# Second-layer expert weights issued from GpSimd's DMA queue, first-layer weights from SyncE's

## The chip, the cores and the metric

The kernel runs on one core of a Trainium2 chip. The metric is the time of the whole program on the device in microseconds (us), as the median of several executions. A trace of one profiled execution stands beside it. Engines are named as the profile names them: PE is TensorE, PEld its weight load, DVE is VectorE, ACT is ScalarE, POOL is GpSimd and SP is SyncE. SP computes nothing here: it issues DMAs. Its DMAs go to the queue that the profile calls q1, hardware_dynamic. DMAs that POOL issues go to q0, software_dynamic. Both queues are served by the same 16 DMA engines of the core.

## The reference

One inference step of a decoder layer on 304 tokens (16 meta tokens, 256 of a prompt, 8 sequences of 4): a layer norm, a mixer of three parallel head groups with one projection in and one out, and then a mixture of 32 experts, of which every token takes 4. The stage that matters here is that last one:

```python
top_val, top_idx = lax.top_k(logits, TOP_K)               # 4 of 32
def expert_block(args):
    xb, e = args
    hid = xb @ lp["moe_w1"][e] + lp["moe_b1"][e]          # 1024 x 2048
    gate = jnp.minimum(hid[:, :D_FF], SWIGLU_LIMIT)
    lin = jnp.clip(hid[:, D_FF:], -SWIGLU_LIMIT, SWIGLU_LIMIT)
    act = gate * jax.nn.sigmoid(SWIGLU_ALPHA * gate) * (lin + 1.0)
    return act @ lp["moe_w2"][e] + lp["moe_b2"][e]        # 1024 x 1024
```

All is float32. An expert has 8 MB of first-layer weights (w1) and 4 MB of second-layer weights (w2), and all 32 experts' weights are read once.

## The kernel before

The program is written engine by engine, with semaphores between the engines set by hand. The first 180 us are the mixer and the router. After that the experts are worked through in 16 pairs. Each expert of a pair takes up to 64 tokens (`CAP`).

**Pieces and slots.** The weights come in pieces of 2 MB, 128 partitions by 16 KB. An expert has `PIECES` = 6 of them: 4 of w1 (`W1P`) and 2 of w2. A pair is `PAIR` = 12 pieces, always in this order, and in this text they are numbered 0 to 11 within their pair: 0 to 3 are w1 of the first expert, 4 to 7 are w1 of the second, 8 and 9 are w2 of the first, 10 and 11 are w2 of the second. SBUF has a ring of `SLOTS` = 8 slots of one piece each. The pieces go through the slots in turn, so a piece may be requested once the piece eight before it has been used. PE counts used pieces on the semaphore `w_used`, and `room(k)` is the wait for it. The loader, `load_group`, loads two pairs per call (`GROUP` = 4 experts) and is called eight times, seven of them in a loop. SP issues all of the pieces, in order, into its one queue. The first eight are issued during the mixer (`load_first`, L454). All signals are per pair of slots: `w_full` for the first piece of two, `w_half` for the second.

**PE's order within a pair** (`pair`, L1870):

1. `first_layer(0, ...)` with pieces 0 to 3 (L1886). In its middle, after half of piece 1, stands `gather(1)`, which picks token columns for a later pair (L1855).
2. `combine`, which adds the pair before to the output (L1863, L1868), with `biases(1)` (L1770) in the middle of it.
3. `first_layer(1, ...)` with pieces 4 to 7. Between pieces 5 and 6 stands `inner(0)`, the transposes of the first expert's activations (L1911).
4. `gather(0)` (L1855), `biases(0)` (L1770), and the transposes of `put` (L1953).
5. `second_layer(0, ...)` with pieces 8 and 9 (L1901), `inner(1)` (L1911) between them, and `second_layer(1, ...)` with pieces 10 and 11 (L1901).

Before each piece PE waits for its `w_full` or `w_half`. After it PE counts `w_used` up.

**POOL.** It makes constants at the start, issues some small loads and the stores of the mixer's states, clears buffers at about 150 us, and then has nothing to do until two multiplications at the very end (L651, L652).

**The end.** After the last pair PE adds the last outputs (L1981, L1992). Then come the last layer norm on DVE and ACT, and the stores. SP issues the last norm's parameters, `ln2`, to the ring's first slots (L527, L528) once the last expert's first layer has been read. These follow the weights in q1.

Of the kernel before, what the change touches and what calls it, by code (L numbers as in the profile page):

```python
# [40 lines left out]
NE, TOPK = 32, 4  # L41
# [15 lines left out]
PIECES = 6  # L57
W1P = 4
PAIR = 2 * PIECES
SLOTS = 8  # L60
GROUP = 4
# [3 lines left out]
PASSES = -(-TOUT // CAP)  # L65
# [52 lines left out]
def build_kernel(nc, x_prompt, x_sample, state_conv_a, state_rglru, state_conv_b, state_gla, meta_tokens, ln0_g, ln0_b,  # L118
# [4 lines left out]
    with ExitStack() as ctx:  # L123
        def sb(name, shape, dt=F32):
            return ctx.enter_context(nc.sbuf_tensor(name, shape, dt))

        def sem(name):
            return ctx.enter_context(nc.semaphore(name))
# [18 lines left out]
        npass = sb("npass", [P, 1], I32)  # L147
# [173 lines left out]
        ld_moe = sem("ld_moe")  # L321
        w_full = [sem(f"w_full{s}") for s in range(SLOTS // 2)]
        w_half = [sem(f"w_half{s}") for s in range(SLOTS // 2)]
        w_used = sem("w_used")
        var_ready, std_ready = sem("var_ready"), sem("std_ready")
        ln0_stats, xhat_ready, h0_ready = sem("ln0_stats"), sem("xhat_ready"), sem("h0_ready")
# [21 lines left out]
        mask_ready, routed, y_started = sem("mask_ready"), sem("routed"), sem("y_started")  # L348
# [48 lines left out]
        def w2_piece(e, s):  # L397
            return moe_w2[0, bass.ds(e, 1), s * 4 * P:(s + 1) * 4 * P, :].rearrange("a (p t) c -> p (a t c)", t=4)

        def slots(s, n):  # L400
            return ring[:, s * SLOT:(s + n) * SLOT]
# [3 lines left out]
        def _(sp):  # L405
# [79 lines left out]

            def load_group(e, n, first=0):

                def expert(i):
                    return e + i if isinstance(e, int) else sp.snap(e + i)

                def room(k):
                    sp.wait_ge(w_used, PIECES * n + k - SLOTS + 1)

                for q in range(2):
                    for j in range(2):
                        for c in range(2):
                            k = PAIR * q + W1P * j + 2 * c
                            if k < first:
                                continue
                            ei = expert(2 * q + j)  # L500
                            src = [w1_half(ei, c, h) for h in range(2)]
                            room(k)
                            sp.dma_start(slots(k % SLOTS, 1), src[0]).then_inc(w_full[k // 2 % 4], 16)
                            room(k + 1)
                            sp.dma_start(slots(k % SLOTS + 1, 1), src[1]).then_inc(w_half[k // 2 % 4], 16)
                    for j in range(2):
                        k = PAIR * q + 2 * W1P + 2 * j
                        ei = expert(2 * q + j)
                        src = [w2_piece(ei, c) for c in range(2)]
                        room(k)  # L510
                        sp.dma_start(slots(k % SLOTS, 1), src[0]).then_inc(w_full[k // 2 % 4], 16)
                        room(k + 1)
                        sp.dma_start(slots(k % SLOTS + 1, 1), src[1]).then_inc(w_half[k // 2 % 4], 16)

            load_group(0, 0, SLOTS)
            with sp.Fori(1, NE // GROUP) as g:
# [3 lines left out]
            n_pass = sp.value_load(npass[0:1, 0:1], min_val=1, max_val=PASSES)  # L520
# [22 lines left out]
        def _(pool):  # L543
# [56 lines left out]
            for b in range(2):  # L600
                r = slice(NE * b, NE * b + NE)
# [29 lines left out]
            for n in range(NSEQ):  # L631
                r = WB - 1 + n * DSEQ
# [12 lines left out]
            st.do(pool.memset(posm[:, :, PASSES * NE:], -1.0), moe_cleared)  # L645
            st.do(pool.memset(eout[:, :, :], 0.0), moe_cleared)
            st.do(pool.memset(putT[:, :], 0.0), moe_cleared)

            pool.wait_ge(ld_lnq, 16 * 8)
            pool.wait_ge(sample_normed, 1)  # L650
# [841 lines left out]
        def _(pe):  # L1492
# [377 lines left out]
            def pair(q, gi, pi, first=False):  # L1870
                def first_layer(j, k0, k1):

                    for k in range(k0, k1):
                        f = (PAIR * q + W1P * j) // 2 + k // 4
                        if k % 4 == 0:
                            pe.wait_ge(w_full[f % 4], 16 * (gi * 3 + f // 4 + 1))
                        if k % 4 == 2:
                            pe.wait_ge(w_half[f % 4], 16 * (gi * 3 + f // 4 + 1))
                        if j == 0 and k < 4 and first:
                            pe.wait_ge(xT_first, k + 1)  # L1880
                        elif j == 0 and k % 4 == 0:
                            pe.wait_ge(xT_ready, 2 * pi + k // 4)
                        for b in range(2):
                            for h in range(2):
                                c = f % 4 * 2 * SLOT + k % 4 * MB1 + (2 * b + h) * 512
                                ins = pe.matmul(bank[b][64 * h:64 * h + 64, :], xT[:, q, k, j * CAP:(j + 1) * CAP],  # L1886
                                                ring[:, c:c + 512], start=False, stop=k == KT - 1)
                        if k % 2 == 1:
                            ins.then_inc(w_used, 1)

                def second_layer(j, k0, k1):

                    f = (PAIR * q + 2 * W1P + 2 * j) // 2
                    for k in range(k0, k1):
                        if k == 0:
                            pe.wait_ge(w_full[f % 4], 16 * (gi * 3 + f // 4 + 1))
                        if k == 4:
                            pe.wait_ge(w_half[f % 4], 16 * (gi * 3 + f // 4 + 1))
                        for h in range(2):
                            c = f % 4 * 2 * SLOT + k * D + h * 512  # L1900
                            ins = pe.matmul(bank[OUT_BANK[j]][64 * h:64 * h + 64, :],  # L1901
                                            actT[:, j, k % 4, (k // 4) * CAP:(k // 4 + 1) * CAP],
                                            ring[:, c:c + 512], start=k == 0, stop=k == KT - 1)
                        if k % 4 == 3:
                            ins.then_inc(w_used, 1)

                def inner(j):

                    pe.wait_ge(act_ready, 2 * pi + j + 1)
                    for k in range(4):  # L1910
                        ins = pe.transpose(bank[3][:, k * P:(k + 1) * P], l1[:, k:512:4], ident[:, :])  # L1911
                    ins.then_inc(actT_full, 1)

                first_layer(0, 0, 3)
                if first:
                    pe.wait_ge(xT_first, 4)
                gather(1)
                if first:
                    first_layer(0, 3, 6)
                    pe.wait_ge(gates_ready, 1)  # L1920
                    for t in range(3):
                        ins = pe.transpose(bank[3][0:NE, t * P:(t + 1) * P], gates[:, t, :], ident[:, :])
                    ins.then_inc(putT_full, 1)
                    first_layer(0, 6, KT)
                else:
                    first_layer(0, 3, KT)

                pe.wait_ge(putT_ready, pi + 1)
                pe.wait_ge(out_ready, 4 * pi + 1)
                combine(pi, 0)  # L1930
                combine(pi, 1)
                pe.wait_ge(bsel_ready, 2 * pi + 2)
                pe.wait_ge(g1_ready, 2 * pi + 1)
                pe.wait_ge(l1_ready, 2 * pi + 1)
                biases(1)
                pe.wait_ge(xT_ready, 2 * pi + 1)
                for c in range(2, NCOMB):
                    combine(pi, c)
                first_layer(1, 0, 4)
                inner(0)  # L1940
                first_layer(1, 4, KT)

                pe.wait_ge(pick_ready, pi + 3)
                pe.wait_ge(y_added, NCOMB * pi + 4)
                gather(0)
                pe.wait_ge(bsel_ready, 2 * pi + 3)
                pe.wait_ge(g1_ready, 2 * pi + 2)
                pe.wait_ge(l1_ready, 2 * pi + 2)
                biases(0)
                pe.wait_ge(put_ready, 2 * pi + 2)  # L1950
                pe.wait_ge(actT_ready, 2 * pi + 1)
                for t in range(3):
                    ins = pe.transpose(bank[3][:, t * P:(t + 1) * P], put[:, t, :], ident[:, :])  # L1953
                ins.then_inc(putT_full, 1)
                pe.wait_ge(y_added, NCOMB * pi + NCOMB)
                second_layer(0, 0, 4)
                pe.wait_ge(putT_ready, pi + 2)
                inner(1)
                second_layer(0, 4, KT)
                pe.wait_ge(actT_ready, 2 * pi + 2)  # L1960
                second_layer(1, 0, KT)

            for q in range(2):
                pair(q, 0, q, first=q == 0)
            pe.wait_ge(routed, 1)
            n_pass = pe.value_load(npass[0:1, 0:1], min_val=1, max_val=PASSES)
# [63 lines left out]
```

## Time and profile before

| | before |
|---|---|
| time, median of 3 runs | 1119.58 us (1119.24 to 1119.7) |
| the profiled execution's own time | 1117.23 us |
| its span in the trace | 1115.4 us |
| TensorE clock over the span | 0.993 of full speed |
| PE busy | 1074.2 us (96%) |
| DVE, ACT, POOL busy | 375.1, 164.1, 40.8 us |
| expert stage, first pair's first matmul to last pair's last | 180.9 to 1096.3 us |
| moved by DMA | 425.71 MB, of it 1.75 MB on q0 |

The span is what the instructions of the trace cover. The execution's own time is 1.8 us longer. "Busy" counts an engine's instructions, not how well they use it. "Idle before" in a row of the timeline is the time in which PE had nothing to do just before the row, with what ended it.

### The profile page before, as it was taken

The page shows a single profiled execution, that of the slowest core. Times are in us where ns is not written, and L with a number is a line of the kernel's source. Part 1 is how long each engine was busy: PE and PEld are TensorE (multiplying, and loading weights), DVE is VectorE, ACT ScalarE, POOL GpSimd, SP SyncE. Part 2 cuts the span into 40 slices and gives each one's busy share as a digit, 9 for nine tenths or more (in the row PEclk, how much of TensorE's full clock was granted, in tenths as well). Part 3 has the DMA queues.
Part 4 walks back from the last instruction along what each step waited for, and adds up shares of the span by engine and source line. Part 5 has one row for each costly group of instructions (what it writes and reads, how often), then busy time and mean ns, then how long its engine had stood idle before and what let it go on. Part 6 is the DMA issues. An engine that isn't in the chain of part 4 may idle for free.

```text
span 1115.4 us, 14027 instructions
## 1 busy us (share of the span) xinstructions
PE 1074.2 (96%) x5443; PEld 467.2 (42%) x5443; DVE 375.1 (34%) x941; ACT 164.1 (15%) x314; POOL 40.8 (4%) x101
## 2 busy tenths in 40 slices
PE   7999889999999999999999999999999999999996
PEld 4667545343434343434343333333333343434342
DVE  4797645313131313131313131223232313122134
ACT  4165622100100010001000100010101010101002
POOL 8000300000000000000000000000000000000000
PEclk9999989999999999999999999999999999999998
DMA  9534637999999999999999999999999999999993
GB/s 291 198 150 160 268 124 264 405 428 430 425 430 430 425 430 426 429 428 428 432 427 430 426 430 431 426 431 426 430 428 428 432 426 430 426 430 431 427 430 127
DMA packets 41642, 425.71 MB, mean 382 GB/s; under 512 B 6617, under 2 KB 13150, under 8 KB 17033
## 3 DMA queue, kind: packets, MB, share of 16 engines
q1 hardware_dynamic: 39729, 423.62, 90.6%
q0 software_dynamic: 1888, 1.75, 0.6%
q8 instruction: 16, 0.26, 0.1%
q14 instruction: 9, 0.07, 0.0%
HBM read 423.39 MB, written 2.17 MB: 382 GB/s over the span
## 4 chain that ended last, share of the span: by engine, by line
PE 73%; DMA 22%; DVE 2%; ACT 1%; POOL 1%; issue 0%; SPq 0%; DVEq 0%
PE bank L1886 34%; DMA ring<-in_moe_w_dram 20%; PE bank L1901 11%; PE bank L1507 7%; PE bank L1855 6%; PE bank L1868 5%; PE bank L1770 2%; PE bank L1534 1%; DMA out_dram<-ring 1%; PE bank L1911 1%; PE bank L1863 1%; PE bank L1739 1%; PE bank L1512 0%; DMA xt<-in_x_prompt_dram 0%; PE bank L1953 0%
## 5 line engine op out<-in xcount | busy, mean ns | idle before, releaser
L1886 PE MATMUL bank<-ring,hT 128*64 128x512 f32 x2048 | 454.9, 595 | 16.0 <-DMA ring<-in_moe_w_dram 16.0
L1886 PEld LDWEIGHTS bank<-ring,hT 128*64 128x64 f32 x2048 | 141.6, 137 | 300.3 <-issue 267.0
L1901 PE MATMUL bank<-ring 128*64 128x512 f32 x1024 | 226.8, 595 | 0.0
L1405 DVE TENSOR_SCALAR ring<-bank 128x512 f32<-128x512 f32 x32 | 22.1, 691 | 311.8 <-PE bank L1886 311.8
L1901 PEld LDWEIGHTS bank<-ring 128*64 128x64 f32 x1024 | 70.7, 137 | 132.6 <-issue 126.3
L1855 PEld LDWEIGHTS bank<-ring 128*128 128x128 f32 x768 | 88.1, 192 | 26.0 <-issue 26.0
L1422 DVE COPY ring<-bank 64x512 f32<-64x512 f32 x32 | 22.2, 694 | 219.3 <-PE bank L1901 219.3
L1855 PE MATMUL bank<-ring 128*128 128x128 f32 x768 | 94.2, 279 | 0.0
L1355 DVE TENSOR_SCALAR hT<-bank,ring 128x128 f32<-128x128 f32 x128 | 43.6, 402 | 130.4 <-PE bank L1855 130.4
L898 ACT ACTIVATE ring<-ring 128x512 f32<-128x512 f32 x32 | 20.1, 630 | 380.4 <-DVE ring L1405 380.4
L1868 PE MATMUL bank<-ring 128*128 128x512 f32 x128 | 63.5, 618 | 0.0
L902 ACT ACTIVATE ring<-bank 128x512 f32<-128x512 f32 x32 | 19.1, 597 | 248.4 <-PE bank L1911 248.4
L1507 PE MATMUL bank<-hT,ring 128*128 128x304 f32 (+1 forms) x208 | 53.4, 415 | 0.0
L1368 DVE TENSOR_TENSOR xt<-xt,bank 128x512 f32<-128x512 f32 x64 | 43.9, 686 | 5.8 <-PE bank L1868 5.5
L1507 PEld LDWEIGHTS bank<-hT,ring 128*128 128x128 f32 x208 | 39.2, 190 | 12.6 <-issue 0.4
L913 ACT ACTIVATE ring<-bank 64x512 f32<-64x512 f32 x32 | 18.9, 589 | 148.4 <-PE bank L1901 148.4
L1868 PEld LDWEIGHTS bank<-ring 128*128 128x128 f32 x128 | 21.7, 189 | 34.9 <-issue 34.9
L1770 PE MATMUL bank<-ring 32*64 32x512 f32 x264 | 35.9, 613 | 0.0
L651 POOL TENSOR_TENSOR ring<-ring 128x256 f32<-128x256 f32 x1 | 0.7, 722 | 958.9 <-ACT ring L930 958.9
L1739 PE MATMUL bank<-ring 128*128 128x512 f32 x64 | 32.6, 668 | 0.0
L1911 PEld LDWEIGHTS bank<-ident,ring 128*128 128x128 f32 x128 | 18.0, 210 | 26.0 <-issue 26.0
L1416 DVE TENSOR_SCALAR ring<-io,ring 128x64 f32<-128x64 f32 x96 | 24.1, 308 | 0.0
(322 smaller groups left out, 619.0 us busy)
## 6 DMA issues: line engine op xcount, KB each, us to landing
ring<-in_moe_w_dram SPq DMA_DIRECT2D x192, 2048.0 KB, 29.5
ring<-in_w_in_dram SPq DMA_DIRECT2D x5, 1536.0 KB, 13.4
ring<-in_w_out_dram SPq DMA_DIRECT2D x2, 2048.0 KB, 11.2
ring<-in_w_in_dram SPq DMA_DIRECT2D x1, 2048.0 KB, 13.7
xt<-in_x_prompt_dram SPq DMA_DIRECT2D x2, 512.0 KB, 4.3
lnbc<-in_ln_g_dram SPq DMA_DIRECT2D x2, 512.0 KB, 12.5
lnbc<-in_ln_b_dram SPq DMA_DIRECT2D x2, 512.0 KB, 12.8
ring<-in_state_gla_dram POOLq DMA_DIRECT2D x4, 144.0 KB, 5.5
```

Of the source, the lines that this page charges most:

```text
L1355: ins = dve.tensor_scalar(xT[:, parity, 4 * b + k, :], bank[(2, 5)[b]][:, k * 2 * CAP:(k + 1) * 2 * CAP], ln1c[:, 0, 4 * b + k:4 * b + k + ...
L1368: dve.tensor_tensor(dst, dst, bank[COMB_BANK[c]][:, :], ALU.add).then_inc(y_added, 1)
L1416: ins = dve.tensor_scalar(put[:, t, j * CAP:(j + 1) * CAP], io64[:, :], posm[:, t, bass.ds(n, 1)], gates[:, t, bass.ds(e, 1)], ALU.is_equa ...
L1422: dve.tensor_copy(eout[64 * j:64 * j + 64, 1, :], bank[OUT_BANK[j]][64:128, :]).then_inc(out_ready, 1)
L1507: ins = pe.matmul(out, a, b, start=n == 0, stop=n == len(pairs) - 1)
L1739: ins = pe.matmul(bk(f"P{t}{c}")[:, :], yT[:, k, cols[t][0]:cols[t][1]], wout[:, k, c * 512:(c + 1) * 512], start=k == 0, stop=k == KT - 1)
L1770: pe.matmul(bank[b][64 * h:64 * h + 64, :], bsel[e0:e0 + NE, j, :], b1_sb[e0:e0 + NE, h, :], start=True, stop=False)
L1855: ins = pe.matmul(out, xh[:, t, k * P:(k + 1) * P], pick[:, t, :], start=t == 0, stop=t == 2)
L1868: pe.matmul(out[:, :], putT[:, t * P:(t + 1) * P], eout[:, h, :], start=True, stop=True).then_inc(comb_full, 1)
L1886: ins = pe.matmul(bank[b][64 * h:64 * h + 64, :], xT[:, q, k, j * CAP:(j + 1) * CAP], ring[:, c:c + 512], start=False, stop=k == KT - 1)
L1901: ins = pe.matmul(bank[OUT_BANK[j]][64 * h:64 * h + 64, :], actT[:, j, k % 4, (k // 4) * CAP:(k // 4 + 1) * CAP], ring[:, c:c + 512], star ...
L1911: ins = pe.transpose(bank[3][:, k * P:(k + 1) * P], l1[:, k:512:4], ident[:, :])
```

## The change

SP's loader issues only the w1 pieces, with the same semaphores as before. POOL gets a loader of its own, `load_second`, which issues the w2 pieces. It stands behind POOL's clearing of the buffers and ahead of its two last multiplications. The w2 pieces have semaphores of their own, `w2_full` and `w2_half`. PE waits for those in `second_layer`, and the counts that it waits for are adapted. The slots, the order of the pieces in the ring and the `w_used` count at which each may be requested stay as they are. Nothing changes in what PE, DVE and ACT compute.

```diff
@@ load_group, on SP
-                    for j in range(2):
-                        k = PAIR * q + 2 * W1P + 2 * j
-                        ei = expert(2 * q + j)
-                        src = [w2_piece(ei, c) for c in range(2)]
-                        room(k)
-                        sp.dma_start(slots(k % SLOTS, 1), src[0]).then_inc(w_full[k // 2 % 4], 16)
-                        room(k + 1)
-                        sp.dma_start(slots(k % SLOTS + 1, 1), src[1]).then_inc(w_half[k // 2 % 4], 16)
...
@@ GpSimd, behind the memset of putT
+            def load_second(e, n):
+
+                def room(k):
+                    pool.wait_ge(w_used, PIECES * n + k - SLOTS + 1)
+
+                for q in range(2):
+                    for i in range(2):
+                        k = PAIR * q + 2 * W1P + 2 * i
+                        ei = e + 2 * q + i if isinstance(e, int) else pool.snap(e + (2 * q + i))
+                        src = [w2_piece(ei, c) for c in range(2)]
+                        room(k)
+                        pool.dma_start(slots(k % SLOTS, 1), src[0]).then_inc(w2_full[k // 2 % 4], 16)
+                        room(k + 1)
+                        pool.dma_start(slots(k % SLOTS + 1, 1), src[1]).then_inc(w2_half[k // 2 % 4], 16)
+
+            load_second(0, 0)
+            with pool.Fori(1, NE // GROUP) as g:
+                load_second(GROUP * g, GROUP * g)
...
@@ second_layer, on PE
                         if k == 0:
-                            pe.wait_ge(w_full[f % 4], 16 * (gi * 3 + f // 4 + 1))
+                            pe.wait_ge(w2_full[f % 4], 16 * (gi + 1))
                         if k == 4:
-                            pe.wait_ge(w_half[f % 4], 16 * (gi * 3 + f // 4 + 1))
+                            pe.wait_ge(w2_half[f % 4], 16 * (gi + 1))
```

On SP, the program around the first call of the loader, before. L454 are the last two of the eight early pieces, L503 and L505 issue w1 pieces, L511 and L513 w2 pieces:

```order
L454 DMA ring<-in_moe_w1_dram 128x4096 [waits bank_full]
L454 DMA ring<-in_moe_w1_dram 128x4096
L511 DMA ring<-in_moe_w2_dram 128x4096 [waits w_used]
L513 DMA ring<-in_moe_w2_dram 128x4096 [waits w_used]
L511 DMA ring<-in_moe_w2_dram 128x4096 [waits w_used]
L513 DMA ring<-in_moe_w2_dram 128x4096 [waits w_used]
L503 DMA ring<-in_moe_w1_dram 128x4096 [waits w_used]
L505 DMA ring<-in_moe_w1_dram 128x4096 [waits w_used]
```

The same place on SP in the changed kernel, whose lines are shifted a little (L456 for L454, L502 for L503, L504 for L505):

```order
L456 DMA ring<-in_moe_w1_dram 128x4096 [waits bank_full]
L456 DMA ring<-in_moe_w1_dram 128x4096
L502 DMA ring<-in_moe_w1_dram 128x4096 [waits w_used]
L504 DMA ring<-in_moe_w1_dram 128x4096 [waits w_used]
L502 DMA ring<-in_moe_w1_dram 128x4096 [waits w_used]
L504 DMA ring<-in_moe_w1_dram 128x4096 [waits w_used]
L502 DMA ring<-in_moe_w1_dram 128x4096 [waits w_used]
```

The four w2 pieces are gone from SP's order, here and once in every pair, so that in q1 a w1 piece of the next pair follows directly on the last one of this pair.

On POOL, after the clearing of the buffers, in the changed kernel (L651 and L653 are now the two DMAs of `load_second`):

```order
L637 MEMSET ring 128x1024
L638 MEMSET ring 128x384
L651 DMA ring<-in_moe_w2_dram 128x4096 [waits w_used]
L653 DMA ring<-in_moe_w2_dram 128x4096 [waits w_used]
L651 DMA ring<-in_moe_w2_dram 128x4096 [waits w_used]
L653 DMA ring<-in_moe_w2_dram 128x4096 [waits w_used]
L651 DMA ring<-in_moe_w2_dram 128x4096 [waits w_used]
```

Before, the multiplication for the last norm (L651) followed directly behind these clearings. Now all 64 w2 pieces stand between them.

## Rows read from the trace of the kernel before

**Rows 1.** The page: DMA queues (packets, MB, share of 16 engines) and issues.
```profile
q1 hardware_dynamic: 39729, 423.62, 90.6%
q0 software_dynamic: 1888, 1.75, 0.6%
ring<-in_moe_w_dram SPq DMA_DIRECT2D x192, 2048.0 KB, 29.5
```

**Rows 2.** Busy time by stretch; the last three columns: PEclk, DMA share, GB/s.
```profile
260.00:316.00 56.00, 56.00 (x285) 22.20 (x283) 15.02 (x38) 5.41 (x8) 0.00 (x0) 1.00 1.01 427
700.00:758.70 58.70, 56.40 (x287) 22.03 (x285) 14.99 (x37) 5.40 (x8) 0.00 (x0) 1.00 1.01 428
1043.50:1092.50 49.00, 48.88 (x251) 19.81 (x251) 14.30 (x36) 3.53 (x6) 0.00 (x0) 1.00 1.00 424
1080.00:1085.00 5.00, 5.00 (x29) 1.58 (x27) 2.04 (x8) 0.49 (x1) 0.00 (x0) 1.00 1.03 439
```

**Rows 3.** Timeline of PE, end of the 15th pair and the last pair.
```profile
1038.81 3.65 PE L1886 MATMUL bank<-ring,hT 128*64 128x512 f32 x16 [1.15 <-DMA ring<-in_moe_w_dram]
1043.62 1.94 PE L1886 MATMUL bank<-ring,hT 128*64 128x512 f32 x8 [1.16 <-DMA ring<-in_moe_w_dram]
1045.49 2.94 PE L1855 MATMUL bank<-ring 128*128 128x128 f32 x24
1048.37 8.80 PE L1886 MATMUL bank<-ring,hT 128*64 128x512 f32 x40
...
1070.21 7.09 PE L1886 MATMUL bank<-ring,hT 128*64 128x512 f32 x32
1077.23 2.94 PE L1855 MATMUL bank<-ring 128*128 128x128 f32 x24
...
1081.60 3.65 PE L1901 MATMUL bank<-ring 128*64 128x512 f32 x16
...
1085.87 10.52 PE L1901 MATMUL bank<-ring 128*64 128x512 f32 x48
1096.32 1.98 PE L1981 MATMUL bank<-xt,ident 128*128 128x512 f32 x4
```

**Rows 4.** Waits of PE for the weights, whole span (us, times, longest).
```profile
PE bank L1886 <- DMA ring<-in_moe_w_dram: 16.0, 14, 1.2
```

**Rows 5.** SP's timeline (the last piece's issue, then ln2), and landing of L527.
```profile
1057.35 0.33 SPq L513 DMA_DIRECT2D ring<-in_moe_w_dram  x1
1078.07 0.35 SPq L527 DMA_DIRECT2D ring<-in_ln_g_dram  x1
DMA to landing us min/median/max: 15.2/15.2/15.2
```

**Rows 6.** DMA issues between 8 and 30 us, KB each, us to landing.
```profile
ring<-in_w_in_dram SPq DMA_DIRECT2D x1, 64.0 KB, 14.9
ring<-in_state_gla_dram POOLq DMA_DIRECT2D x4, 144.0 KB, 5.5
```

**Rows 7.** DMA between 96 and 106 us, then between 125 and 140 us.
```profile
q0 software_dynamic: 32, 0.21, 5.1%
out_dram<-in_state_conv_b_dram POOLq DMA_DIRECT2D x1, 208.0 KB, 6.0
...
out_dram<-ring POOLq DMA_DIRECT2D x4, 144.0 KB, 12.1
```

**Rows 8.** Busy time by stretch around 125 to 150 us, columns as in rows 2.
```profile
125.00:130.00 5.00, 4.79 (x68) 2.66 (x58) 3.61 (x9) 3.33 (x11) 4.52 (x9) 1.00 1.01 433
135.00:140.00 5.00, 3.28 (x15) 1.86 (x13) 0.30 (x2) 4.09 (x5) 1.61 (x3) 1.00 1.01 421
140.00:145.00 5.00, 3.80 (x20) 2.19 (x21) 0.00 (x0) 1.12 (x2) 0.00 (x0) 0.52 1.00 421
145.00:150.00 5.00, 5.00 (x11) 2.25 (x10) 1.17 (x2) 0.00 (x0) 1.40 (x4) 0.80 0.24 82
```

**Rows 9.** Timelines: POOL's DMA instructions, then PE's wait at 141 us.
```profile
19.80 2.54 POOL L573 DMA_DIRECT2D ring<-in_state_gla_dram  x4
...
141.20 1.06 PE L1761 MATMUL bank<-wr,hT 128*32 128x32 f32 x16 [2.92 <-ACT hT L844]
```

More of the change, by code:

```diff
@@ L323, in build_kernel @@
         w_half = [sem(f"w_half{s}") for s in range(SLOTS // 2)]
+        w2_full = [sem(f"w2_full{s}") for s in range(SLOTS // 2)]
+        w2_half = [sem(f"w2_half{s}") for s in range(SLOTS // 2)]
         w_used = sem("w_used")
@@ L486, in load_group @@
             def load_group(e, n, first=0):
-                def expert(i):
-                    return e + i if isinstance(e, int) else sp.snap(e + i)
                 def room(k):
@@ L494, in load_group @@
                 for q in range(2):
-                    for j in range(2):
+                    for i in range(2):
                         for c in range(2):
-                            k = PAIR * q + W1P * j + 2 * c
+                            k = PAIR * q + W1P * i + 2 * c
                             if k < first:
                                 continue
-                            ei = expert(2 * q + j)
+                            ei = e + 2 * q + i if isinstance(e, int) else sp.snap(e + (2 * q + i))
                             src = [w1_half(ei, c, h) for h in range(2)]
@@ L505, in load_group @@
                             sp.dma_start(slots(k % SLOTS + 1, 1), src[1]).then_inc(w_half[k // 2 % 4], 16)
-                    for j in range(2):
-                        k = PAIR * q + 2 * W1P + 2 * j
-                        ei = expert(2 * q + j)
-                        src = [w2_piece(ei, c) for c in range(2)]
-                        room(k)
-                        sp.dma_start(slots(k % SLOTS, 1), src[0]).then_inc(w_full[k // 2 % 4], 16)
-                        room(k + 1)
-                        sp.dma_start(slots(k % SLOTS + 1, 1), src[1]).then_inc(w_half[k // 2 % 4], 16)
             load_group(0, 0, SLOTS)
@@ L647, in _ @@
             st.do(pool.memset(putT[:, :], 0.0), moe_cleared)
+            def load_second(e, n):
+                def room(k):
+                    pool.wait_ge(w_used, PIECES * n + k - SLOTS + 1)
+                for q in range(2):
+                    for i in range(2):
+                        k = PAIR * q + 2 * W1P + 2 * i
[8 more added lines that the diff above has]
+                load_second(GROUP * g, GROUP * g)
+            pool.wait_ge(routed, 1)
+            n_pass = pool.value_load(npass[0:1, 0:1], min_val=1, max_val=PASSES)
+            with pool.If(n_pass > 1):
+                with pool.Fori(1, n_pass) as r:
+                    with pool.Fori(0, NE // GROUP) as g:
+                        load_second(GROUP * g, NE * r + GROUP * g)
             pool.wait_ge(ld_lnq, 16 * 8)
@@ L1875, in first_layer @@
                         if k % 4 == 0:
-                            pe.wait_ge(w_full[f % 4], 16 * (gi * 3 + f // 4 + 1))
+                            pe.wait_ge(w_full[f % 4], 16 * (gi * 2 + f // 6 + 1))
                         if k % 4 == 2:
-                            pe.wait_ge(w_half[f % 4], 16 * (gi * 3 + f // 4 + 1))
+                            pe.wait_ge(w_half[f % 4], 16 * (gi * 2 + f // 6 + 1))
                         if j == 0 and k < 4 and first:
@@ L1895, in second_layer @@
                         if k == 0:
-                            pe.wait_ge(w_full[f % 4], 16 * (gi * 3 + f // 4 + 1))
+                            pe.wait_ge(w2_full[f % 4], 16 * (gi + 1))
                         if k == 4:
-                            pe.wait_ge(w_half[f % 4], 16 * (gi * 3 + f // 4 + 1))
+                            pe.wait_ge(w2_half[f % 4], 16 * (gi + 1))
                         for h in range(2):
```

## Prediction

> **What bounds the kernel now.** I read the page first. It shows PE busy for 96% of the span, but also 192 pieces of 2 MB that all go through q1, with a median of 29.5 us from issue to landing [rows 1]. So two resources are near their limit, and the table by stretches decides between them. Early in the expert stage a pair takes 56.0 us, PE is busy in all of it, and the 16 DMA engines are busy too: 427 GB/s at a share of 1.01 [rows 2]. Later, as between 700 and 758.7 us, a pair takes 58.7 us, PE is busy for 56.4 of them, and the DMA rate is the same 428 GB/s. A pair's 12 pieces are 25.17 MB, and 25.17 MB in 58.7 us is 429 GB/s. So a pair costs 56.0 us on PE and 58.7 us on the DMA engines, 4.89 us a piece. The ring starts full and its lead of eight pieces lasts for the first half of the stage. After that PE waits. The list of waits has 16.0 us in 14 waits, none above 1.2 us [rows 4]. They come at pieces 0 and 1 of each pair [rows 3].
>
> The DMA engines set the time to the very end. Piece 1 of the last pair was there at 1043.6 us [rows 3]. Ten pieces were left, 48.9 us, so the last one should land at 1092.5. Two other rows agree: `ln2`, queued behind it, was issued at 1078.1 and landed 15.2 us later, at 1093.3, and its 512 KB are 1.2 us of transfer [rows 5]. PE reaches that last piece 7.0 us into the block of 10.5 us that starts at 1085.9, so at 1092.9 [rows 3]. It is then done at 1096.3. **Only 3.5 us of PE's expert work lie behind the last landing.** Behind 1096.3 lies the tail of 19.1 us, which the change leaves alone.
>
> **The change, part by part.**
>
> *Issue cost.* 64 issues of 0.33 us leave SP [rows 5]. On POOL such an instruction takes about 0.63 us (four in 2.54) [rows 9], so 64 take 41 us on an engine that is idle through the stage. Both engines wait for the same counts of `w_used` as before. Hardly any DMA is issued earlier or later, and one more microsecond is covered by the pieces that are queued ahead. I cost this at 0. Without that cover it would be 0.3 us for a piece at which PE waits. Behind POOL's waits only its two last multiplications are queued; the last w2 piece was issued at 1057 [rows 5], and they belong to the norm behind 1096.3. 0 as well.
>
> *Total transfer.* Bytes are the same. If the engines still move 428 GB/s whenever anything is queued, the last landing stays near 1092.5, since the engines never run dry: with eight slots, something is always requested while PE is the one that waits.
>
> *Order of arrival.* Here is the price. Today q1 hands over pieces in the order in which PE needs them. With two queues it matters how an engine shares itself between them. Three rows tell. Between 8 and 30 us a 64 KB load in q1 took 14.9 us, since it stood behind others, while 144 KB loads in q0 took 5.5 us [rows 6]: q0 does not stand behind q1. At 125 to 140 us, 144 KB stores of 384-byte rows in q0 ran beside pieces in q1 and took 12.1 us [rows 7]. They are 384 rows, 24 for each engine. If an engine alternates row by row with q1's 16 KB rows (4.89 us for 128 rows on 16 engines is 0.61 us each), 24 turns take 14.7 us, near the 12.1. And q0 does not cut rows small: its 208 KB moved in 32 packets [rows 7], 6.6 KB each on average, or 13 KB if one packet on each of the 16 engines is a completion signal. A 16 KB row of w2 should then take turns with a 16 KB row of w1, one to one. The Trainium skill (DMA: Bandwidth & Descriptors, Queues, rings and completion order) says the same: each engine goes round robin between its queues, packet by packet. Its rules for kernel authors add that spreading DMAs over issuing engines doesn't help bandwidth; by that rule alone the change would be worth 0, and the harm comes only with the order.
>
> So while w2 is queued, w1 gets half the rate, 9.8 us a piece. Follow the last pair. Piece 8 is requested as piece 0 is released, pieces 9 to 11 as 1 to 3 are. At that time pieces 4 to 7 of w1 are not there yet. Four w2 pieces and about four w1 pieces share the engines one to one, so both queues run empty at nearly the same time: piece 7 of w1, which used to land four pieces (19.6 us) ahead of piece 11, now lands within one piece of the end, at 1092.5 less 0 to 4.9 us. Behind piece 7 PE still has its own 3.5 us, `gather(0)`, `biases(0)` and the `put` transposes (1077.2 to 1081.6, 4.4 us), and the second layers (1081.6 to 1096.3, 14.7 us) [rows 3]: 22.6 us in place of 3.5. That is +19.1 less 0 to 4.9, so **+14.2 to +19.1 us**.
>
> In the pairs before, the same thing moves PE's waits from pieces 0 and 1 to piece 7. There they cost nothing of their own, as the DMA engines set the pace and keep working. The lead at piece 7 is smaller, so the waits begin earlier, and in sum they grow by what the end grows, from 16 to some 31 us.
>
> *Clock.* Today's waits of 1.2 us leave the granted clock at 1.00 [rows 2, 3]. After a wait of 2.92 us at 138 to 141 us [rows 9] it was 0.52 for 5 us and 0.80 for 5 more, between the levels of 1.2 and 2.4 GHz [rows 8]; at full speed that is 2.4 + 1.0 = 3.4 us of work lost. If waits at piece 7 bunch to some 4 us in every other pair, the last pair may pay 0 to 3.4 us. Earlier pairs have 2.7 us of slack for it.
>
> *Sum.* 14.2 to 22.5 us. I take +16, from the middle of the first range with little for the clock, since half of the pairs would have short waits. Span 1115.4 + 16 = 1131.4, execution 1133.2; the median runs 2.35 us above the profiled execution, so **1135.6 us**.
>
> **Rivals.**
>
> *Rate falls with two queues.* Nothing in the trace mixes 16 KB rows of both queues. The nearest rows are the stretches with q0's stores beside pieces: 433 and 421 GB/s [rows 8]. Between 181 and 1092 us, 184 pieces need 900 us, so 421 (-1.6%) costs 15 us more and 433 (+1.2%) gives 11 back: 1151 or 1125. Some loss beyond 1% I give 0.15, around 1147.
>
> *Faster: the two queues keep the engines fuller.* With x% more rate the end moves by 16 - 9x us, so it turns at 1.8%, 436 GB/s. The best short stretch showed 439 (2.5%) [rows 2], which would give -6.5, 1113 us. The floor is PE's own 56.0 us a pair: 180.9 + 56.7 + 15 x 56.0 = 1077.6 in place of 1096.3, so 1101 us. Against it: over whole pairs the rate is 427 and 428, with shares that are already 1.01 [rows 2]. 0.07. The same page of the Trainium skill puts the ceiling at 435 GB/s; at that rate the sum would be +1.6 us, not faster.
>
> *No change.* The engines might in effect serve requests as they arrive, or keep w1 ahead in the last pair. Then all is as before, 1119.6. [rows 6] speak against it. 0.11.
>
> *Very uneven turns.* If q0 got everything first, piece 7 would land last: +19.1, inside my sum. If q1 got nearly everything, w2 would starve, and each pair would wait for at least one w2 piece, 4.9 us, beyond the 2.7 us of slack: +35 us, 1155, or more. The 5.5 us of [rows 6] speak against it. 0.03.
>
> *My forecast*, sharing in turns at about today's rate: 0.64, on its own 1130 to 1143.
>
> **How the numbers follow.** 0.2% is 2.2 us, about what a measurement of this kernel can tell from none. Slower: 0.64 + 0.15 + 0.03, and 0.01 of the rest, 0.83. Same: 0.10. Faster: 0.07. The range for 8 in 10 reaches from the no-change case to a rate loss of 1.5%: 1119.5 to 1150. It leaves out the faster case, half of no change, starving and the deepest rate losses.
>
> **What would show it.** Right: q0 carries 64 pieces, 134 MB; the DMA rate stays 427 to 429 GB/s; PE waits for pieces at the line of the first layer's matmuls, late in it, 25 to 35 us in all, not at pieces 0 and 1; in the last pair a wait ends with piece 7 and 19 to 23 us of expert work follow it; the stage ends near 1112. The tail stays 19 us. Wrong: a rate off 428 by over 1%, waits at the second layer's matmuls (w2 starved), or DMA engines idle while PE waits.

## The result

| | before | changed |
|---|---|---|
| median of 4 runs | 1119.64 us (1119.24 to 1122.15) | 1139.17 us (1133.47 to 1140.32) |
| the profiled execution's own time, its span | 1117.23 us, 1115.4 us | 1138.43 us, 1136.8 us |
| first matmul of the expert stage | 180.9 us | 183.4 us |
| end of the last second layer | 1096.3 us | 1112.9 us |
| the stage between them | 915.5 us | 929.5 us |
| behind the stage, to the end of the span | 19.1 us | 23.9 us |

The changed kernel is slower: the ratio is 1.0159, with a 95% interval from 1.0122 to 1.0197, or 18 us (the medians lie 19.5 us apart). The forecast was 1135.6 us, in a range from 1119.5 to 1150.0. The two traced spans differ by 21.4 us: 14.1 us in the stage, 4.8 us behind it, and 2.5 us ahead of it, where nothing was changed and where the time moves from run to run. When the changed kernel was run a second time, one execution of it took 2834 us in place of 1137 to 1139, and no figure here uses it.

The page of the changed kernel, queues (packets, MB, share of 16 engines) and issues of weight pieces (KB each, us to landing):

```profile
q1 hardware_dynamic: 30513, 289.40, 61.1%
q0 software_dynamic: 11104, 135.97, 28.5%
...
ring<-in_moe_w_dram SPq DMA_DIRECT2D x128, 2048.0 KB, 19.9
ring<-in_moe_w_dram POOLq DMA_DIRECT2D x64, 2048.0 KB, 17.6
```

The change does what it says: 64 pieces of w2, 134 MB, have moved to q0 [rows 1]. Busy time by stretch, with granted clock, DMA share and GB/s in the last columns; 260 to 1060 us is the body of the expert stage, the rest is its end:

```profile
260.00:1060.00 800.00, 779.65 (x3880) 306.14 (x3878) 204.43 (x503) 66.09 (x104) 28.03 (x53) 0.99 1.01 428
1085.00:1090.00 5.00, 3.73 (x18) 1.06 (x16) 0.00 (x0) 0.60 (x1) 0.00 (x0) 1.00 1.00 426
...
1094.00:1095.00 1.00, 1.00 (x10) 1.00 (x11) 1.00 (x2) 0.33 (x1) 0.00 (x0) 1.00 0.23 98
```

The rate is what it was [rows 2], 428 GB/s, and at about 1094 us nearly all of the weights are there: the DMA engines fall from a share of 1.00 to 0.23. The last piece is complete a little later. Its issue on POOL with its way to landing, in us, and then the landing of the last piece of before, whose issue at 1057.35 is in [rows 5]:

```profile
1072.68 0.53 POOL L653 DMA_DIRECT2D ring<-in_moe_w_dram  x1 [2.89 <-PE bank L1902]
DMA to landing us min/median/max: 23.6/23.6/23.6
...
DMA to landing us min/median/max: 35.2/35.2/35.2
```

So the last weights landed at 1096.3 us where they had landed at 1092.6. That is 3.7 us later, of which 2.5 us are the later start of the stage. What has grown is PE's work behind that landing: 3.8 us before, 16.6 us now. PE's timeline at the end, where [rows 3] were; L1902 is the first layer's matmul now, L1917 the second's, L1871 `gather`:

```profile
1085.07 3.65 PE L1902 MATMUL bank<-ring,hT 128*64 128x512 f32 x16
1090.24 3.65 PE L1902 MATMUL bank<-ring,hT 128*64 128x512 f32 x16 [1.51 <-DMA ring<-in_moe_w_dram]
1093.82 2.94 PE L1871 MATMUL bank<-ring 128*128 128x128 f32 x24
...
1098.19 3.65 PE L1917 MATMUL bank<-ring 128*64 128x512 f32 x16
...
1102.46 10.52 PE L1917 MATMUL bank<-ring 128*64 128x512 f32 x48
1112.91 1.98 PE L1997 MATMUL bank<-xt,ident 128*128 128x512 f32 x4
```

PE waits for piece 7 of w1, and then has 22.7 us to go. The six other waits for weights, from the same timeline:

```profile
445.39 5.35 PE L1902 MATMUL bank<-ring,hT 128*64 128x512 f32 x16 [3.84 <-DMA ring<-in_moe_w_dram]
...
562.91 6.63 PE L1902 MATMUL bank<-ring,hT 128*64 128x512 f32 x16 [3.64 <-DMA ring<-in_moe_w_dram]
...
678.54 3.65 PE L1902 MATMUL bank<-ring,hT 128*64 128x512 f32 x16 [0.48 <-DMA ring<-in_moe_w_dram]
...
739.71 5.27 PE L1902 MATMUL bank<-ring,hT 128*64 128x512 f32 x16 [4.97 <-DMA ring<-in_moe_w_dram]
...
855.96 5.18 PE L1902 MATMUL bank<-ring,hT 128*64 128x512 f32 x16 [2.45 <-DMA ring<-in_moe_w_dram]
...
974.63 5.57 PE L1902 MATMUL bank<-ring,hT 128*64 128x512 f32 x16 [4.97 <-DMA ring<-in_moe_w_dram]
```

All are at piece 7, in pairs two apart as a rule, and the first comes at 445 us, not at 686. And they have a second price. Sixteen matmuls take 3.65 us at the full clock; behind five of the seven waits they took 5.18 to 6.63 us. The table by stretches shows why, here for the first two:

```profile
445.00:450.00 5.00, 4.61 (x14) 1.44 (x16) 0.00 (x0) 0.00 (x0) 0.00 (x0) 0.66 1.00 426
563.00:568.00 5.00, 5.00 (x12) 1.39 (x14) 0.00 (x0) 0.00 (x0) 0.00 (x0) 0.50 1.02 433
```

The granted clock was 0.66 and 0.50 there. The page's rows for the matmuls of the first layer, before and then changed (busy us, mean ns | idle us before them):

```profile
L1886 PE MATMUL bank<-ring,hT 128*64 128x512 f32 x2048 | 454.9, 595 | 16.0 <-DMA ring<-in_moe_w_dram 16.0
...
L1902 PE MATMUL bank<-ring,hT 128*64 128x512 f32 x2048 | 464.3, 605 | 21.9 <-DMA ring<-in_moe_w_dram 21.9
```

They are busy for 464.3 us where it was 454.9, with the same instructions. So of the time that PE loses to late weights, 21.9 us are waits and 9.4 us a lower clock.

Last, the 4.8 us behind the stage. Everything there runs 16.6 us later than before, up to the last store. Then SP waits for another engine. The closing instructions of the program, of the changed kernel (shortest, middle and longest in ns, then the start in us):

```profile
L123 POOLq DRAIN  x1: 10253/10253/10253, 1126.3 to 1126.3; - x1
...
L123 SPq COMPARE_BRANCH  x1: 41/41/41, 1131.7 to 1131.7; - x1
```

and of the kernel before:

```profile
L123 POOLq DRAIN  x1: 5019/5019/5019, 1109.7 to 1109.7; - x1
...
L123 SPq COMPARE_BRANCH  x1: 41/41/41, 1115.0 to 1115.0; - x1
```

POOL ends each program with a drain. Before, it took 5.0 us and was over at 1114.7, just ahead of SP's end at 1115.0. Now it takes 10.3 us, to 1136.6, and SP waits for it from 1131.7 on. I had not thought of it.

### The profile page after: what moved, and what is told of

The parts are those of the page before. It is cut to its first block, busy times and chain, and to the rows that moved or that the text cites. A ratio compares the mean times of both kernels' runs of the same rounds, so it can differ in the third digit from the quotient of the medians.

```text
span 1136.8 us, 14041 instructions
## 1 busy us (share of the span) xinstructions
PE 1085.2 (95%) x5443; PEld 472.4 (42%) x5443; DVE 375.2 (33%) x941; ACT 164.1 (14%) x314; POOL 74.6 (7%) x165
## 4 chain that ended last, share of the span: by engine, by line
PE 71%; DMA 24%; DVE 2%; ACT 1%; POOL 1%; issue 0%; SPq 0%; DVEq 0%
PE bank L1902 25%; DMA ring<-in_moe_w_dram 22%; PE bank L1917 20%; PE bank L1523 6%; PE bank L1871 6%; PE bank L1884 3%; PE bank L1786 2%; PE bank L1927 2%; PE bank L1550 1%; DMA out_dram<-ring 1%; PE bank L1755 1%; PE bank L1969 1%; PE bank L1528 0%; PE bank L1879 0%; PE bank L1777 0%
## 5 line engine op out<-in xcount | busy, mean ns | idle before, releaser
L1902 PE MATMUL bank<-ring,hT 128*64 128x512 f32 x2048 | 464.3, 605 | 21.9 <-DMA ring<-in_moe_w_dram 21.9
L1902 PEld LDWEIGHTS bank<-ring,hT 128*64 128x64 f32 x2048 | 144.2, 139 | 311.4 <-issue 271.0
L1917 PE MATMUL bank<-ring 128*64 128x512 f32 x1024 | 226.8, 595 | 0.0
L1917 PEld LDWEIGHTS bank<-ring 128*64 128x64 f32 x1024 | 70.7, 137 | 132.5 <-issue 130.6
L1871 PEld LDWEIGHTS bank<-ring 128*128 128x128 f32 x768 | 88.1, 192 | 26.3 <-issue 26.3
L1871 PE MATMUL bank<-ring 128*128 128x128 f32 x768 | 94.2, 279 | 0.0
L651 POOL DMA_DIRECT2D ring<-in_moe_w_dram x32 | 17.0, 530 | 746.9 <-PE bank L1902 746.9
L918 ACT ACTIVATE ring<-bank 128x512 f32<-128x512 f32 x32 | 19.1, 597 | 248.4 <-PE bank L1927 248.4
L653 POOL DMA_DIRECT2D ring<-in_moe_w_dram x32 | 16.9, 529 | 141.5 <-PE bank L1902 141.5
## 6 DMA issues: line engine op xcount, KB each, us to landing
ring<-in_moe_w_dram SPq DMA_DIRECT2D x128, 2048.0 KB, 19.9
lnbc<-in_ln_b_dram SPq DMA_DIRECT2D x2, 512.0 KB, 12.2
```

Source lines behind the costliest of these rows:

```text
L1871: ins = pe.matmul(out, xh[:, t, k * P:(k + 1) * P], pick[:, t, :], start=t == 0, stop=t == 2)
L1917: ins = pe.matmul(bank[OUT_BANK[j]][64 * h:64 * h + 64, :], actT[:, j, k % 4, (k // 4) * CAP:(k // 4 + 1) * CAP], ring[:, c:c + 512], star ...
```

## The experiments

Three things were to be told apart. The **order theory**: w1's pieces arrive late because the DMA engines take turns between the queues. The **queue theories**: q0, its issue or the new signals cost something by themselves. And, for the size, where in the stage the loss is made. For the last I stepped the ring's rule through the 16 pairs by arithmetic: a piece is requested when the piece eight before has been used, a transfer takes 4.89 us of the engines' time, halved while both queues hold something, and PE needs the times of [rows 3]. The expectations call it stepping.

Stage and drain are those of each run's profile, so of one execution; time against the kernel before is the ratio of the timed runs, times 1119 us. The 95% intervals of that last column reach 1.9 to 6.2 us to either side, so it is the length of the stage that carries the argument.

| run | stage, us | POOL's drain, us | against before, us |
|---|---|---|---|
| before | 915.5 | 5.02 | |
| changed | 929.5 | 10.25 | +17.8 |
| changed_again | 930.0 | 10.25 | +19.9 |
| one_queue_split_signals | 915.6 | 5.02 | +1.0 |
| all_on_gpsimd | 919.9 | 7.96 | +7.7 |
| two_queues_first_half | 918.0 | 7.64 | +4.4 |
| queues_swapped | 929.0 | 2.09 | +14.9 |
| last_pair_in_order | 927.3 | 9.92 | +17.5 |
| last_pair_two_queues | 935.6 | 5.35 | +22.3 |
| before_64_tiny_loads | 915.5 | 10.25 | +3.6 |
| two_queues_second_half | 933.0 | 7.63 | +17.8 |
| last_four_pairs_in_order | 921.0 | 8.94 | +6.4 |

The first matmul of the stage moved between 178.5 and 184.2 us from run to run, whatever the kernel. The stage's length is compared for that reason. It came out as 915.5, 915.6 and 915.5 us for the three kernels that keep all pieces in order in q1, and as 929.5 and 930.0 us for the changed kernel. I take it as good to 2 us or so, since part of the first requests does not move along.

How the engines share themselves can be read from the traces too. The queues while both hold w1 and w2 pieces of the last pair, 1072 to 1078 us in the changed kernel, then 1064 to 1070 us with the queues exchanged (packets, MB, share of 16 engines):

```profile
q0 software_dynamic: 94, 1.28, 50.5%
q1 hardware_dynamic: 90, 1.26, 49.4%
...
q0 software_dynamic: 88, 1.36, 53.2%
q1 hardware_dynamic: 91, 1.23, 48.2%
```

Each queue gets half of the engines' time, whichever of the two holds w1. And the transfers as a whole are not what differs between the runs: in all twelve traces the last packet of the weights ended 911 to 914 us behind the stage's first matmul, while the stage's length ran from 915.5 to 935.6 us.

**One queue, split signals.** SP's loader issues all pieces again, w2 with its own semaphores:

```diff
+                for q in pairs:
+                    for k in range(PAIR * q, PAIR * q + PAIR, 2):
+                        r = k - PAIR * q
+                        one = r < 2 * W1P
...
+                        full, half = ((w_full, w_half) if one else (w2_full, w2_half))
+                        room(k)
+                        sp.dma_start(slots(k % SLOTS, 1), src[0]).then_inc(full[k // 2 % 4], 16)
...
-            load_second(0, 0)
```

> All pieces are issued by SP in the old order into q1; w2 keeps its own semaphores. Order theory (w1's pieces arrive late because w2 shares the DMA engines with them): the time of before, 1119.6 us within 2, waits of PE at pieces 0 and 1 of a pair again, 14 to 18 us in all. Rival, the new signals and PE's changed waits cost something: it stays above 1130.

Ratio 1.0009 (0.9984 to 1.0033). The stage and the waits are back, 16.1 us at pieces 0 and 1:

```profile
PE bank L1878 <- DMA ring<-in_moe_w_dram: 16.1, 14, 1.2
```

The signals cost nothing that these runs can tell.

**All on POOL.** From the ninth piece on POOL issues everything in the old order; SP's loader is gone. PE waits for w1 on semaphores of POOL's own. Here and below, words behind # are added for this text:

```diff
+            load_all(0, 0, SLOTS)                       # on POOL
+            with pool.Fori(1, 8) as g:
+                load_all(GROUP * g, GROUP * g)
-            load_group(0, 0, SLOTS)                     # on SP
-            with sp.Fori(1, NE // GROUP) as g:
-                load_group(GROUP * g, GROUP * g)
```

> All pieces from the ninth on are issued by POOL, in the old order, into q0 alone. Order theory: 1119.6 us, up to 2.4 more, as ln2 (1 MB on q1) no longer stands behind the last pieces but shares with them; stage rate 427 to 429 GB/s. Rival, the software queue is slower or its issue late: with one third of the pieces it cost 19 us, so with all of them some 50, 1150 or more.

Ratio 1.0069 (1.0049 to 1.0089), +7.7 us, more than the 2.4 expected and far less than 30. The body of the stage is that of before, at 428 GB/s through q0 alone, with the same waits of 1.2 us at pieces 0 and 1. What is new comes at the very end, at the last piece:

```profile
1085.38 7.16 PE L1924 MATMUL bank<-ring 128*64 128x512 f32 x32
1094.60 5.35 PE L1924 MATMUL bank<-ring 128*64 128x512 f32 x16 [2.06 <-DMA ring<-in_moe_w_dram]
```

It came late while `ln2`, now in the other queue, landed beside it: the first half of `ln2` took 10.0 us from issue to landing, where it had taken 15.2 behind the weights [rows 5]. The block behind the wait ran 1.7 us longer, at a granted clock of 0.66. The stage is 4.4 us longer in all; the drain adds 2.2. So the software queue carries the whole stream as fast as the hardware queue does. What it costs is at the ends.

**Two queues in the first half only.** The changed kernel for eight pairs, the old order for the rest, w2 with a second set of semaphores from there on:

```diff
+            with sp.Fori(1, 4) as g:
+                load_all(GROUP * g, GROUP * g, 0, '1')                   # w1 only
+            with sp.Fori(4, 8) as g:
+                load_all(GROUP * g, GROUP * g, 0, '12', (0, 1), True)    # all
```

> The first eight pairs take w2 through q0 as in the changed kernel, the last eight have all pieces from SP in order. Order theory: the late w1 pieces of the first half fall into the ring's lead and the second half restores the order, so 1119.6 us within 3, no trace left. Rival, each piece through q0 or each pair with two queues has its price: half of the 19.5 us, 1129.

Ratio 1.0039 (1.0021 to 1.0058), +4.4 us, of which the drain explains 2.3 and 2.5 are in the stage. PE waited at piece 7 at 440 and 558 us, as in the changed kernel, and from 868 us on at pieces 0 and 1, as in the kernel before. So eight pairs with two queues leave little behind if order follows, though not "no trace". The time alone, 4.4 us, lies between the two theories; stage and drain apart decide it.

**Queues swapped.** w1 from POOL, w2 from SP, each list as in the changed kernel.

> w1 from POOL through q0 (from the ninth piece on), w2 from SP through q1. Order theory: engines take turns whichever queue is whose, so as the changed kernel, 1134 to 1140 us, with waits at the first layer's pieces. Rival, the software queue is served worse than the hardware queue: w1 would starve more and it would be slower than 1145; if the software queue were served better, 1120 to 1130.

Ratio 1.0133 (1.0094 to 1.0172), +14.9 us, median 1131.75. That is a little below what was expected of the order theory, 1134 to 1140, and the drain accounts for it: it took 2.1 us here and was hidden, where it had added 4.8 us to the changed kernel. The stage is 929.0 us, as in the changed kernel, with eight waits of 1.0 to 4.4 us at piece 7. It does not matter which queue is whose.

**Where the loss is made.** Four kernels restore or break the order in part of the pairs. They differ from the first-half kernel in the bounds of the loops, and the last pair is written out on its own where it is treated apart.

```diff
+            with sp.Fori(1, 7) as g:                                     # last_pair_in_order
+                load_all(GROUP * g, GROUP * g, 0, '1')
+            load_all(28, 28, 0, '1', (0,))
+            load_all(28, 28, 0, '12', (1,), True)                        # all of the last pair
```

> As the changed kernel, but in the last of the 16 pairs SP issues all pieces in the old order. Expert stage of before: 915.5 us from first to last matmul, of the changed kernel 929.5. If only the end pays for the late w1 pieces, as the prediction had it, the stage is back at 915 to 918. Rival: PE's lateness at piece 7 is built up in the pairs before and carried along, and the last pair adds only the rest; stepping the ring's rule through the pairs gives a recovery of 4 us, so 924 to 927 us. A third, apart from the stage: POOL's closing drain, which took 10.3 us in the changed kernel and 5.0 before, if it grows with POOL's DMAs by 0.08 us each, is 9.9 us with 60 w2 pieces.

The stage is 927.3 us: of the 14 us only 2.2 come back by the first run of the changed kernel, 2.6 by the second (930.0 us, below), close to the 924 to 927 us of the stepping. This refutes what the prediction said of the earlier pairs.

> All pieces in order from SP, except the four w2 pieces of the last pair, which POOL issues into q0. Order theory: those four share with w1 pieces 1 to 7 that PE is waiting for already, so the whole loss comes in one pair: stage 930 to 935 us, waits of 5 to 7 us at w1 pieces of the last pair alone. Rival, a price per w2 piece on q0 or per pair: one sixteenth of the loss, stage 916 to 917. POOL's drain, at 0.08 us a DMA: 5.4 us, hidden.

The stage is 935.6 us: four pieces out of 64, in one pair, lose 20 us, more than all 64 do. PE's timeline in that pair:

```profile
1062.65 5.30 PE L1903 MATMUL bank<-ring,hT 128*64 128x512 f32 x16 [6.12 <-DMA ring<-in_moe_w_dram]
...
1082.23 5.75 PE L1903 MATMUL bank<-ring,hT 128*64 128x512 f32 x16 [5.28 <-DMA ring<-in_moe_w_dram]
...
1090.18 3.65 PE L1903 MATMUL bank<-ring,hT 128*64 128x512 f32 x16 [1.52 <-DMA ring<-in_moe_w_dram]
...
1095.04 3.65 PE L1903 MATMUL bank<-ring,hT 128*64 128x512 f32 x16 [1.20 <-DMA ring<-in_moe_w_dram]
```

The waits come at pieces 3, 5, 6 and 7; two of them are shorter than the 5 to 7 us expected. The last is over at 1095.04, and the stage ends at 1117.71, 22.7 us later. This is the walk through the last pair that the prediction made.

> The first eight pairs have all pieces from SP in order, the last eight take w2 through q0. Order theory: the loss is made in the pairs before the end, so all of it comes back, stage 928 to 932 us (915.5 before, 929.5 in the changed kernel). Rival, a price per pair with two queues: half of it, 922 to 923. POOL's drain with 32 w2 pieces 7.6 us, ending about 2.3 us behind the last store: 1135 us.

The stage is 933.0 us, a little above the 928 to 932 expected: the whole loss and 3 us more. In the pair in which the second queue sets in, PE waited for 12.2 us in four waits.

> Twelve pairs take w2 through q0, the last four have all pieces from SP in order. With the last pair in order the stage was 927.3 us, with the last eight 918. If PE works its lateness off at the 2.7 us a pair by which its own work is shorter than the transfers, four pairs give back 10 to 11 of the 14: stage 919 to 921. Rival, recovery all at once as soon as order is restored in more than one pair, or only with the lead of the ring built up anew: stage 916 or 927. POOL's drain with 48 w2 pieces 8.9 us, 3.6 us behind the last store.

The stage is 921.0 us, at the upper edge of what was expected: against the 930.0 us of the second run four pairs in order give back 9 us, where one gave 2.6 and eight 12. That is 2.2 to 2.6 us a pair for the first four, close to the 2.7 us by which PE's own 56.0 us are shorter than a pair's 58.7 us of transfer [rows 2].

**The drain.** The kernel before, with 64 loads of 128 bytes that nothing reads, issued by POOL between 59 and 90 us. They go into unused rows of the tile of `smask`, which is made larger for them, and POOL waits for them ahead of its last two multiplications:

```diff
+            for n in range(64):
+                r, c = SAMP + 16 * (n % 4), 2 * (n // 4)
+                pool.dma_start(smask_all[r:r + 16, c:c + 2], x_prompt[0, r:r + 16, c:c + 2]).then_inc(ld_scrap, 16)
```

> The kernel before, with 64 loads of 128 bytes added on POOL at 60 us, where it and the DMA engines are idle. They load what nothing reads. If POOL's closing drain grows with the number of DMAs that it has issued, 0.08 us each as the runs so far give between 51, 83 and 115 DMAs, it takes 10.3 us in place of 5.0 and the span ends 5 us later, 1124 us. Rival: the drain depends on the size or time of the DMAs, or on the program's code, and not on their number: drain 5.0 us, 1119.6.

Ratio 1.0032 (1.0013 to 1.0051), +3.6 us. The stage is untouched, 915.5 us, and the drain is that of the changed kernel to 4 ns, over 1000 us after the last of these loads:

```profile
L123 POOLq DRAIN  x1: 10249/10249/10249, 1111.1 to 1111.1; - x1
...
L123 SPq COMPARE_BRANCH  x1: 41/41/41, 1116.5 to 1116.5; - x1
```

So it went with how many DMAs POOL had issued, not with their bytes or with when.

**The changed kernel again**, beside these:

> The changed kernel once more, beside the runs of this job. Stage 929 to 932 us with the first matmul at 178 to 185 us; POOL's drain 10.3 us again if it is fixed by the program, anything from 2 to 10 if it varies from run to run. 1134 to 1140 us.

Stage 930.0 us, drain 10.25 us, ratio 1.0178 (1.0123 to 1.0234). One thing differs. Its waits fall in other pairs, and the last is in the 15th:

```profile
1031.82 6.08 PE L1902 MATMUL bank<-ring,hT 128*64 128x512 f32 x16 [4.24 <-DMA ring<-in_moe_w_dram]
```

In the last pair PE waits for nothing, and the stage ends at 1112.90 all the same. From the end of that wait PE runs without another: 81.1 us to the end of the stage, which are 2.4 us of lower clock, the 22.7 us behind a piece 7, and the 56.0 us of one more pair. What PE is late by was settled before the last pair.

## Why the prediction was right, and where it was not

**What bounds the kernel.** Right. The rate between 260 and 1060 us was 428 GB/s in every kernel, whichever queues carried it. Counted from the stage's first matmul, the last piece landed after 911.7 us before and after 912.9 us in the changed kernel.

**Order of arrival: one to one.** Right, and it carries the forecast. Swapping the queues leaves the stage as it was, and joining them in either queue gives the old stage back but for its last piece. While both queues held weights, q0 had 50.5% and q1 49.4% of the engines' time. The trace agrees here with what the Trainium skill says of an engine's turns (DMA: Bandwidth & Descriptors, Queues, rings and completion order). The Trainium skill's rule that spreading DMAs over engines does not help bandwidth (the same page, Rules for kernel authors) agrees too, at 428 GB/s on one queue or two. But the order of arrival in the last pair is not the whole price.

**The size, +14.2 to +19.1 us.** The stage grew by 14.1 us, 14.5 in the second run: the low end. Piece 7 landed 6.0 us ahead of the last piece in the first run, just beyond the 0 to 4.9 us that gave the range. The reason behind the size failed in one step, "In the pairs before, the same thing moves PE's waits from pieces 0 and 1 to piece 7. There they cost nothing of their own". It holds for the pace of the transfers, which did not change, and for the place of the waits and their earlier start. It fails for PE: if only the last pair's order mattered, putting that pair alone in order would have returned all of it. It returned 2.2 to 2.6 us. With w2 taking turns PE falls behind the DMA engines by more than it did. This takes no more than one pair (20 us, where the second queue sets in with the last one). PE then carries its lateness from pair to pair, with pieces ready in the ring that it is not at yet, and can make it good only at 2.7 us a pair. At the end of the weights the lateness is what is left to do: 16.6 us of PE work in the first run and 17.5 in the second, in place of 3.8. The last pair's own walk, 22.6 us behind piece 7, is right for a pair that takes up the second queue on its own (22.7 us in that run, and in the first run of the changed kernel). But it is not what sets the end in general, as the second run shows, in which PE did not wait in the last pair.

**The waits, "from 16 to some 31 us".** Too high: the waits were 21.9 us, below the 25 to 35 us named as the sign of being right. A lower clock took 9.4 us more, so that late weights cost PE 31.3 us in all; that this sum meets the forecast of the waits alone is chance. The prediction had counted the clock apart, as 0 to 3.4 us in the last pair. In the first run it cost nothing there: that wait was 1.5 us, and the clock stayed at 1.00. No run took the clock's share away by itself, so whether the stage would be shorter without it is not shown.

**Issue cost.** 0, right for the stage. A w2 DMA on POOL took 0.53 us, not 0.63.

**"Behind 1096.3 lies the tail of 19.1 us, which the change leaves alone."** Wrong by 4.8 us. This is the term that was missing, and with it the forecast, +16, becomes +21. That the +16 lies so near the +17.8 of the ratio is in part luck: the stage cost 1.9 us less than the sum and the tail 4.8 us more. POOL's drain was in the trace before, 5.0 us and 0.3 us short of being seen. It was not looked at, because POOL had no work on the path.

Of the rivals, the falling rate and the fuller engines are refuted by the same 428 GB/s, the uneven turns by the shares of the two queues and by the swapped queues, and no change by the time itself.

No version here beats the kernel before. The closest, all in order with split signals, is the same kernel.

## What to carry to other kernels

When a stage is bound by DMA and its buffers are a ring, a second queue added no rate here; it changed the order of arrival, and what was needed next came at half speed while the other queue was full. Count how much work is left behind the last landing, and by how much a period of the consumer is shorter than one of the DMA: the second tells over how many periods a disturbance is worked off, and so whether it matters where it happens. And look at what each engine does after its last instruction: an idle engine's closing work can lie just below the end of the program.

## What the hardware showed that I had not expected

- POOL's closing drain by the number of DMAs added to the 51 that it issues before: 0: 5.02 us, 4: 5.35, 32: 7.64 and 7.63, 48: 8.94, 60: 9.92, 64: 10.25 (three times, once with loads of 128 bytes in place of 2 MB). That is 0.082 us each, to within 0.01 us over these six counts. At 120 it was 2.09 and at 184 it was 7.96, so beyond some count it does not simply go on growing. Why stays open.
- q0 alone carried 184 pieces at 428 GB/s, as q1 does, and the waits in the body of the stage came to 16.2 us against 16.0.
- The granted clock fell to 0.50 to 0.70 for some 5 us after most of PE's waits of 2.1 to 6.1 us, but not after all: one of 3.85 us left the next 16 matmuls at 3.65 us, and one of 2.1 us made them 5.35 us. None of the waits below 2 us did it.
